# First layer of a hybrid decoder step: the norm's squares are summed by TensorE inside the mixing stage

## The reference, cut to what matters

```python
def rmsnorm(x, g):
    xf = x.astype(jnp.float32)
    xf = xf * lax.rsqrt(jnp.mean(xf * xf, axis=-1, keepdims=True) + EPS)
    return (xf * g.astype(jnp.float32)).astype(x.dtype)
...
def layer(x, p_in, pos, attend, C0, n0, m0, buf0, lw):
    B, T, _ = x.shape
    h = rmsnorm(x, lw['norm_mix'])
    z = h @ lw['w_in']
```

## Time and profile before

| | |
|---|---|
| time, median of 3 runs | 3032.24 us (3027.56, 3032.24, 3032.86) |
| the profiled execution: its own time | 3027.98 us |
| its span, first to last instruction | 3026.2 us |
| PE busy | 2858.7 us, 94% of the span |
| DVE, ACT busy | 60%, 41% |
| mean granted TensorE clock | 0.976 |

### The profile page before, as it was taken

One profiled execution on the slowest core, in us unless ns is written; L12 is line 12 of the kernel. 1 busy time (PEld: TensorE's weight loads), 2 busy tenths in 40 slices (PEclk: granted clock), 3 DMA queues, 4 the chain that ended last, 5 costly groups with the idle time before them and its releaser, 6 DMA issues. The chain is left out here.

```text
span 3026.2 us, 49911 instructions
## 1 busy us (share of the span) xinstructions
PE 2858.7 (94%) x20323; PEld 2699.4 (89%) x20323; DVE 1801.6 (60%) x3013; ACT 1228.4 (41%) x2007; POOL 152.6 (5%) x264
## 2 busy tenths in 40 slices
PE   6999989998999999999989999899889999999997
PEld 5999755997999999999989987569889999999997
DVE  5234644577888885445661445445788888744365
ACT  6233423444444454334452342343444444533253
POOL 0000400000110110000000003000000000000000
PEclk9999999999999999999999989999999999999998
DMA  3101243421222146443221022524122222754321
GB/s 132 43 29 50 93 161 107 172 99 51 77 85 81 69 172 237 171 144 131 91 74 43 15 97 85 171 85 179 66 85 70 79 85 72 256 178 166 142 99 71
DMA packets 134375, 326.28 MB, mean 108 GB/s; under 512 B 9978, under 2 KB 75770, under 8 KB 125954
## 3 DMA queue, kind: packets, MB, share of 16 engines
q1 hardware_dynamic: 134146, 323.09, 30.7%
HBM read 271.74 MB, written 51.31 MB: 107 GB/s over the span
## 5 line engine op out<-in xcount | busy, mean ns | idle before, releaser
L236 PE MATMUL psum<-g_tiles,down_units 128*128 128x352 f32 x1056 | 344.4, 326 | 12.4 <-DVE down_units L2611 12.4
L237 PE MATMUL psum<-g_tiles,down_units 128*128 128x352 f32 x1056 | 340.3, 322 | 0.0
L238 PE MATMUL psum<-g_tiles,down_units 128*128 128x352 f32 x1056 | 339.2, 321 | 0.0
L2829 PE MATMUL psum<-t_high,sum_units 128*128 128x264 f32 x1008 | 288.0, 286 | 7.1 <-DVE sum_units L2546 3.8
L2830 PE MATMUL psum<-t_low,sum_units 128*128 128x264 f32 x1008 | 287.7, 285 | 0.0
L2831 PE MATMUL psum<-t_high,sum_units 128*128 128x264 f32 x1008 | 287.0, 285 | 0.0
L2329 ACT ACTIVATE down_units<-down_units_raw 128x1408 fp32r<-128x1408 f32 x96 | 132.4, 1381 | 287.3 <-DMA down_units_raw<-w_down_dram 287.3
L2555 DVE SCALAR_TENSOR_TENSOR conv_sum<-u_padded,vectors,conv_sum 128x1024 f32<-128x1024 f32 x176 | 225.6, 1282 | 12.7 <-ACT conv_sum L2279 11.0
L236 PEld LDWEIGHTS psum<-g_tiles,down_units 128*128 128x128 f32 x1056 | 199.0, 188 | 14.0 <-issue 11.1
L2829 PE MATMUL psum<-h_b,block_units 128*128 128x264 f32 x672 | 194.5, 289 | 14.1 <-ACT norm L2298 14.1
L236 PE MATMUL psum<-h_high,mix_weight_parts 128*128 128x352 f32 x576 | 193.7, 336 | 11.2 <-DVE mix_weight_parts L228 8.1
(11 more groups left out here) (390 smaller groups left out, 7688.6 us busy)
## 6 DMA issues: line engine op xcount, KB each, us to landing
down_units_raw<-w_down_dram SPq DMA_DIRECT2D x96, 704.0 KB, 4.1
block_units_raw<-w_up_dram SPq DMA_DIRECT2D x42, 768.0 KB, 4.6
gated_rows<-conv_sum SPq DMA_DIRECT2D x44, 528.0 KB, 2.7
g_tiles_raw<-gated_rows SPq DMA_DIRECT2D x38, 528.0 KB, 5.0
mix_weight_stage<-w_in_dram SPq DMA_DIRECT2D x18, 1024.0 KB, 4.8
pages<-cache_dram SPq DMA_DIRECT2D x64, 288.0 KB, 4.4
out_weight_stage<-w_out_dram SPq DMA_DIRECT2D x16, 1024.0 KB, 6.9
out_weight_stage<-w_gate_dram SPq DMA_DIRECT2D x16, 1024.0 KB, 4.8
```

Of the source, the lines that this page charges most:

```text
L236: pe.matmul(out, lhs[0], rhs[0], start=first, stop=False)
L237: pe.matmul(out, lhs[0], rhs[1], start=False, stop=False)
L238: return pe.matmul(out, lhs[1], rhs[0], start=False, stop=last)
L2829: pe.matmul(out, w[0], parts[0], start=begin and k == 0, stop=False, skip_group_check=not begin)
```

## The change

`first_squares` and its barrier are gone. In the first layer `mix_projection` now loads x, the constants and the first weight tile itself (the weight tile before the second third of x), and the sum of squares is taken by PE: for each block k ACT squares x into one of two buffers (`first_sq`), and a plain f32 matmul with a 128x128 matrix of ones adds it into a bank of `psum`, so that every partition gets the sum of its token. ACT takes the root of a whole row of 352 from `psum` into `core.norm` (`root_row`), DVE its reciprocal in place (`inverse_row`). The squares and sums of third c+1 stand in ACT's and PE's programs between the blocks k = 1 to 4 of third c. A first root of a small tile of ones loads ACT's table ahead. The first weight tile is split in two halves, between the first blocks. The second layer's branches do the same as before.

```diff
-def first_squares(nc, core, mem, X, columns, constants):
...
+            if not l:
+                def x_third(c):
+                    sp.dma_start(X[:, :, chunk(c)], core.x_in[:, :, chunk(c)]).then_inc(ph["x_loaded"][c], 16)
+                x_third(0)
+                for dst, src in constants[0:2]:
+                    sp.dma_start(dst, src).then_inc(ph["constants_loaded"], 16)
+                sp.dma_start(ring.stage[:, 0, :], core.w_in[0, 0]).then_inc(ph["first_loaded"], 16)
+                x_third(1)
+                x_third(2)
...
+            def inverse_row(c):
+                row = core.norm[:, chunk(c)]
+                dve.wait_ge(ph["root_made"], c + 1)
+                dve.reciprocal(row, row).then_inc(ph["spread_made"], 1)
...
+                inverse_row(0)
+                for c in range(NC):
+                    for k in range(0, KX, 2):
+                        n = KX * c + k
+                        parts.scale(dve, c, k, n, c + 1)
+                        parts.scale(dve, c, k + 1, n + 1, c + 1)
+                        if n == 0:
+                            first_half_low()
+                        if n == 2:
+                            second_half_low()
+                        parts.low(dve, c, k, n)
+                        parts.low(dve, c, k + 1, n + 1)
+                        if c < NC - 1 and k == KX - 2:
+                            inverse_row(c + 1)
...
+            def square(c, k):
+                s = KX * c + k
+                if k == 0:
+                    act.wait_ge(ph["x_loaded"][c], 16)
+                if s >= 2:
+                    act.wait_ge(ph["square_sums"], s - 1)
+                act.activation(first_sq[:, s % 2, :], X[:, k, chunk(c)], ACT.Square).then_inc(ph["sq_made"], 1)
+            def root_row(c):
+                act.wait_ge(ph["square_sums"], KX * (c + 1))
+                act.activation(core.norm[:, chunk(c)], ps[:, B_SQUARES + c % 2, 0:CH], ACT.Sqrt, bias=core.eps,
+                               scale=1.0 / D_MODEL).then_inc(ph["root_made"], 1)
...
+                for k in range(KX):
+                    square(0, k)
+                act.wait_ge(ph["constants_loaded"], 32)
+                root_row(0)
+                act.wait_ge(ph["first_loaded"], 16)
+                first_half_high()
+                for c in range(NC):
+                    for k in range(KX):
+                        parts.high(act, c, k, KX * c + k)
+                        if c == 0 and k == 1:
+                            second_half_high()
+                        if c < NC - 1 and 1 <= k <= 4:
+                            square(c + 1, 2 * k - 2)
+                            square(c + 1, 2 * k - 1)
+                        if c < NC - 1 and k == 5:
+                            root_row(c + 1)
...
+            def square_sum(c, k):
+                s = KX * c + k
+                pe.wait_ge(ph["sq_made"], s + 1)
+                if c == 2 and k == 0:
+                    pe.wait_ge(ph["root_made"], 1)
+                pe.matmul(ps[:, B_SQUARES + c % 2, 0:CH], core.ones, first_sq[:, s % 2, :], start=(k == 0),
+                          stop=(k == KX - 1)).then_inc(ph["square_sums"], 1)
...
+                    if not l and c < NC - 1 and 1 <= k <= 4:
+                        square_sum(c + 1, 2 * k - 2)
+                        square_sum(c + 1, 2 * k - 1)
```

More of the change, by code:

```diff
@@ L568, in mix_groups, with mix_projection @@
     return groups, starts
-def mix_projection(nc, core, mem, X, columns):
+def mix_projection(nc, core, mem, X, columns, constants):
     l = core.l
@@ L673, in _ @@
         def _(pool):
+            if not l:
+                pool.memset(seed[:], 1.0).then_inc(ph["seeded"], 1)
             pool.memset(vTM[:, :, :, M_DV:M_DV + 1], 1.0).then_inc(ph["ones_made"], 1)
@@ L922, in _ @@
+            def root_row(c):
+                act.wait_ge(ph["square_sums"], KX * (c + 1))
+                act.activation(core.norm[:, chunk(c)], ps[:, B_SQUARES + c % 2, 0:CH], ACT.Sqrt, bias=core.eps,
+                               scale=1.0 / D_MODEL).then_inc(ph["root_made"], 1)
+            if l:
+                first_half_high()
+                second_half_high()
                 for k in range(KX):
-                    parts.high(act, c, k, KX * (c - first_third) + k)
-                    if c == 1 and k == 3:
+                    parts.high(act, 1, k, k)
+                    if k == 3:
@@ L925, in _ @@
                         norm.root(act, 2, 1)
-            norm.keep(act, 2, 1)
-            for k in range(KX):
-                parts.high(act, 2, k, LATE + k)
+                norm.keep(act, 2, 1)
+                for k in range(KX):
+                    parts.high(act, 2, k, LATE + k)
+            else:
+                act.wait_ge(ph["seeded"], 1)
+                act.activation(seed[:, 0:2], seed[:, 2:4], ACT.Sqrt)
+                for k in range(KX):
[3 more added lines that the diff above has]
+                act.wait_ge(ph["first_loaded"], 16)
+                first_half_high()
+                for c in range(NC):
+                    for k in range(KX):
+                        parts.high(act, c, k, KX * c + k)
+                        if c == 0 and k == 1:
+                            second_half_high()
+                        if c < NC - 1 and 1 <= k <= 4:
[3 more added lines that the diff above has]
+                            root_row(c + 1)
@@ L1032, in values @@
                 mm.then_inc(ph["upd_done"], 1)
-            if not ready:
-                pe.wait_ge(ph["half_lo"], 1)
+            def square_sum(c, k):
[5 more added lines that the diff above has]
+                          stop=(k == KX - 1)).then_inc(ph["square_sums"], 1)
+            if not l:
+                pe.wait_ge(ph["constants_loaded"], 32)
+                for k in range(KX):
+                    square_sum(0, k)
+            pe.wait_ge(ph["half_lo"], 1)
             for c in range(NC):
                 for k in range(KX):
-                    if not ready and c == 0 and k == KX // 2:
+                    if c == 0 and k == KX // 2:
                         pe.wait_ge(ph["lo_made"], 1)
```

49 lines of the change are left out of this document (29 added, 20 removed).

## The result

The changed kernel takes 3036.07 us (median of 20 runs, 3031.79 to 3045.24) against 3027.58 for the kernel before on the same chip (20 runs, 3019.6 to 3034.18): a ratio of 1.003, with a 95% interval of 1.0021 to 1.0039. It is 8.5 us slower. The profiled execution took 3041.52 us, with a span of 3039.7, 13.5 above the span of before; 4 of the 20 runs lie higher still.

What follows compares the result with a forecast made beforehand. PE, busy 94% of the span, was taken as the bound. The first product 8.8 us earlier, then 17.4 us longer to the second job, gave +8.6 us: 3038.7 us, midway between two bases, range 3032 to 3045.

Steps and rivals of the forecast that it cites:

- The first product: Head of the first layer's mixing stage: PE's first product comes at 23.3 instead of 32.07, 8.8 us earlier.
- The price of a sum: PE's plain f32 sum of squares: two passes of 0.29 us, 0.59 at 2.4 GHz and 1.18 at 1.2.
- The rival in which plain f32 sums run at the products' rate: PE's sums take 0.16 us a pass, so the net is about +3 us, 3031 to 3035; chance 0.03.
- The row reciprocal: DVE's reciprocal of 352 elements, three times on the chain: 2.2 us each, by a straight line from narrower ones.
- The rival in which it streams: DVE's row reciprocal takes 0.42 us instead of 2.2: net +3.3 us, 3031.3 to 3035.5; chance 0.09.
- Block 6's wait: In thirds with sums, PE waits 0.85 us because `root_row` stands ahead of block 6's high part on ACT.
- the boundary's: Between thirds, PE waits 2.45 us for DVE's low part, reciprocal and scaling; expected at two boundaries.
- The thirds: First product to second job: 13.25 + 2.45 + 13.25 + 2.45 + 10.5 = 41.9, plus 2.5 slow clock, 44.4 against 27.0.
- the second rival: The boundary's 2.45 us idle also drops PE's clock, +1.8 us more in the second third: +10.4 to +12; chance 0.13.
- The total: Whole kernel: 17.4 us longer behind the first product less 8.8 us gained ahead of it, net +8.6 us.
- The base: Starting time for the sum: profiled 3027.98 gives 3036.6, median 3032.24 gives 3040.8; the middle, 3038.7, was taken.
- The shift stays to the end: Behind the second job's start all orders are as before and no transfer sets PE's time, so +8.6 us remains.

Runs made afterwards that it cites:

- the second profile: The changed kernel run once more, unchanged, in one set with a kernel that adds nine constant matmuls: 3036.31 us, ratio 1.0025 to the kernel before.
- the one-pass kernel: Changed kernel with squares and ones kept as fp32r, so each sum is one matmul pass: 3030.76 us, ratio 1.0 to the kernel before.
- the kernel with eight buffers: Changed kernel with eight square buffers instead of two, next third's squares and sums behind blocks 0 to 3, root behind block 7's high part: 3026.35 us, ratio 0.9991.
- the nine matmuls: Changed kernel plus nine f32 matmuls of constants into an unread bank behind the first sums, keeping PE busy: 3039.15 us, ratio 1.0026 to the kernel before.
- the kernel whose row streams: Changed kernel with each row's reciprocal replaced by a multiplication with one: 3026.69 us, ratio 0.999 to the kernel before.
- the nine matmuls, again: The changed kernel plus nine constant matmuls behind the first sums, rerun beside the changed kernel: 3033.32 us, ratio 1.002 to the kernel before.
- the early split: Changed kernel with one-pass sums, eight buffers, and the second weight tile's high part behind the last root: 3016.33 us, ratio 0.9962 to the kernel before.

## Why the prediction held, step by step

- **The first product**, forecast at 23.3, came at 23.24 (23.80 in the second profile, whose first sums took 8.13 us and not 7.58). Inside, the sums ended at 17.4 (forecast 17.8), the root took 0.55 (0.46) and the reciprocal 2.35 (2.2).
- **The price of a sum.** Four records, two sums, take 1.34 us; less a fill of 0.25 that is 0.27 a pass, against 0.29 from the earlier trace rows. By the pace it is 0.30: blocks with two sums start 2.15 apart, of which six products at 0.16 are 0.96. The rival in which plain f32 sums run at the products' rate is out; the one-pass kernel shows what it would have been worth, 4.1 us between the products. The formula of the Trainium skill, page "TensorE: Matmul & The Clock Gate", section "Back-to-back issue gap", which has no term for the type, fits the fp32r products of this trace (0.16) and not its f32 passes.
- **The row reciprocal**, taken as a straight line from the earlier trace rows, measured 2347 ns. The line was right and its slope the upper one: 348 + 320 x 6.25 = 2348; I had carried on the lowest part with 5.85. The rival in which it streams is out: a streaming row is 338 ns. The Trainium skill, page "VectorE: DVE Perf Modes", section "First, the fixed hardware budget", says that the reciprocal runs as an iterated division with a repeat count of 8 and gives no time; here the row costs 2347 / 338 = 6.9 times a streaming one, and the measurement decides.
- **Block 6's wait**, forecast 0.85, is 0.62 and 0.63; **the boundary's**, forecast 2.45, is 2.22 and 2.21. Both were sized a little too high, by 0.23. The sum had them as two terms with causes of their own; the kernel with eight buffers showed that both hang on one cause, ACT held back by the sums.
- **The thirds.** Forecast: 18.2 for the first (13.25 + 2.45 + 2.5 of slow clock), 15.7 for the second, 10.5 for the last. Measured: 17.81, 17.38, 10.31. The first product to the second job: 45.50 against 44.4. The term that was mis-sized is the second third, by 1.7 us: **the boundary idle does drop the clock**, to 0.53 for 3.65 us. That was the second rival, with 0.13. It happened behind both boundaries in both profiles of the changed kernel (0.61 and 0.56 over 3.4 us in the second). What it costs is shown by the nine matmuls, where the first boundary's idle is as long and 1.00 follows: their second third takes 15.85 and 15.82, near the forecast's 15.7. The earlier trace rows had shown 2.40 without a fall and 2.47 with one; taking the first for the likely case was the choice that failed. Even the idle of that row, at 76.00 before, is followed by half clock in both profiles of the changed kernel. The last boundary's fall was hidden by the tail, as the rival had it: the last third is 10.31 with or without it.
- **The total.** The local shift is 9.67 in the profiled run, against 8.6 forecast. The median's is 8.5. That forecast and median agree to 0.1 is therefore partly luck: the head came out 1.1 us dearer, 2.2 in the second profile, mostly by a mechanism that had been given 0.13, and the rest of the run moved the sum again, up to 13.5 in the first profile and down to 8.1 in the second.
- **The base.** I took the middle between two bases, 3036.6 and 3040.8. With 20 runs before lies at 3027.58, by the profiled execution's own time; 3036.6 would have been the better number, and 3038.7 is 2.6 high.
- **"The shift stays to the end"** is the step that holds only roughly. Measured at the same matmuls of both traces, counted from the end, the shift in the profiled run is 11.0 us at 80 to 290 us of before, about 8 at 500 to 620, 10.1 at 750 to 1090, 10.7 at 1280 to 1960, 8.7 at 2086, 13.0 from 2270 and 13.4 at the end; in the second profile of the changed kernel 12.3, about 9, 9.1, 8 to 12, 4.2, 8.0 and 8.0. The first step, from 9.7 to 11.0 and from 10.8 to 12.3, is the half clock behind the idle at 85.46 (86.80 in the second profile): the prediction argued that all orders there are as before, and left out that an idle which was there before can now drop the clock. Further on, there are stretches of low granted clock that lie differently: 147.5 us of the record in 23 spells before, 174.2 in 27 and 163.7 in 25 after, of which in each 17.1 in four spells lie in the first 91 us, where the record of before has none. Why one execution gets a spell at a place and another doesn't, no run here shows; that part of the median's scatter stays open.

## What to carry to other kernels

When a small reduction is moved into a full matrix stage, price it as every engine's added slot in that stage: passes by operand type on PE, a non-streaming operation's whole width on the chain of each tile, and the place in the in-order program of the one instruction that waits for the sum. Here the first and the last could be repaired for a few lines (one-pass operands; enough buffers together with the waiting root behind the last high part), the reciprocal stayed as long as it was, and the same idea then won some 12 us instead of losing 8.5. And read an idle that the change creates by what follows it: one of 0.2 or 0.9 us cost only itself here, one of 2.2 mostly also 3.4 us at half clock, which is 1.7 us where PE sets the pace.

## What the runs showed of the hardware that was not expected

- An idle of PE of 2.18 to 2.27 us at a boundary was followed by a granted clock of 0.50 to 0.64 over the next 3.4 us in 9 of 12 places in seven profiles and by 1.00 in the other three, even within one execution (2.22 and 2.21 with the nine matmuls). The six of 0.21 to 1.15 were all followed by 1.00. An idle of 3.87, in the kernel whose row streams, was followed by first products of 0.40 us, the 2.4 GHz kind, and only then by a stretch of 0.61; the six idles of 5.87 to 5.88 were all followed by the slow rate. At the idle of the earlier trace rows at 76.00, the clock fell in five of nine profiles and read 1.00 in four (in the tenth, the early split's, the idle is only 0.39): 1.94 us long with a fall (the nine matmuls, again) and 2.80 without one (one-pass sums). In these runs the length of an idle alone doesn't say which it will be.
- The profiled executions' mean granted clock and time go together: the changed kernel's ran at 0.972 with a span of 3039.7 and at 0.973 with 3034.3, before's at 0.976 with 3026.2. It holds within one kernel too: of the 20 runs of the changed kernel the twelve at 0.973 to 0.975 took 3031.79 to 3036.25, the eight at 0.971 and 0.972 took 3038.02 to 3045.24. So a few us of a span of some 3030 go with the clock of the execution and not with the kernel.
